# The last 32 tiles of a down-projection: from plain fp32 to three products of rounded parts and remainders

## The reference

```python
q = (xb @ w_q).reshape(tb, PEER_HEADS, 2, D_KEY // 2)
s = jnp.einsum('thpc,pnc->thpn', q, sub_keys).astype(jnp.float32)
...
gate = jax.nn.softmax(best_s, axis=-1)
pre = jnp.einsum('thkd,td->thk', u[expert], xb).astype(jnp.float32)
act = jax.nn.gelu(pre, approximate=False) * gate
return jnp.einsum('thk,thkd->td', act.astype(v.dtype), v[expert])
```

## Time and profile before

| what | value |
|---|---|
| median of 3 runs | 1876.55 us (1875.07 to 1878.01) |
| profiled execution, its own time | 1875.91 us |
| its span, first to last instruction | 1874.1 us |
| mean granted TensorE clock | 0.973 |
| PE, PEld, DVE busy | 95%, 81%, 77% of the span |
| ACT, POOL busy | 42%, 34% of the span |
| moved by DMA | 478.22 MB, mean 255 GB/s |
| the down-projection, first matmul to last | 1285.9 to 1860.4 us |

### The profile page before, as it was taken

One profiled execution on the slowest core, in us unless ns is written; L12 is line 12 of the kernel. 1 busy time (PEld: TensorE's weight loads), 2 busy tenths in 40 slices (PEclk: granted clock), 3 DMA queues, 4 the chain that ended last, 5 costly groups with the idle time before them and its releaser, 6 DMA issues.

```text
span 1874.1 us, 26361 instructions
## 1 busy us (share of the span) xinstructions
PE 1777.3 (95%) x9675; PEld 1516.0 (81%) x9675; DVE 1434.5 (77%) x2750; ACT 778.4 (42%) x1555; POOL 644.6 (34%) x409
## 2 busy tenths in 40 slices
PE   6999999989999899999999999978999999999997
PEld 6999776559998899999899999976676666766764
DVE  4433676665678788989999999867888788888787
ACT  3112566553444333333768788522222222222222
POOL 1100000000000133434223366555557566665672
PEclk8999799789999999999999999999999999999998
DMA  6233100002222589989788899999999999999996
GB/s 217 68 131 121 45 1 1 1 1 85 68 77 95 185 305 334 316 307 327 262 276 297 279 387 387 386 400 333 386 389 382 401 387 389 401 402 384 400 379 216
DMA packets 153599, 478.22 MB, mean 255 GB/s; under 512 B 14896, under 2 KB 53808, under 8 KB 149888
## 3 DMA queue, kind: packets, MB, share of 16 engines
q1 hardware_dynamic: 96112, 264.62, 38.7%
q0 software_dynamic: 56928, 208.28, 30.4%
q10 hardware_dynamic: 432, 3.64, 0.5%
HBM read 419.47 MB, written 56.75 MB: 254 GB/s over the span
## 4 chain that ended last, share of the span: by engine, by line
PE 69%; DVE 16%; DMA 8%; ACT 3%; issue 3%; POOL 0%; SPq 0%; ACTq 0%; DVEq 0%
PE ps L1003 17%; PE ps L981 16%; PE ps L633 10%; PE ps L1012 7%; PE ps L918 5%; DMA g_in<-gates_scattered 4%; PE ps L723 3%; DVE hot L1718 3%; DVE w_lo L1339 3%; DVE ring L1737 2%; PE ps L969 2%; PE ps L714 2%; PE ps L766 2%; DMA ring<-u_rows,idx_b 1%; DMA raw<-w_tiles 1%
## 5 line engine op out<-in xcount | busy, mean ns | idle before, releaser
L981 PE MATMUL ps<-md_hi,w_hi 128*128 128x384 f32 x1024 | 358.6, 350 | 36.9 <-DVE w_lo L1339 36.7
L981 PE MATMUL ps<-md_hi,w_lo 128*128 128x384 f32 x1024 | 345.8, 338 | 0.0
L981 PE MATMUL ps<-md_lo,w_hi 128*128 128x384 f32 x1024 | 345.7, 338 | 0.0
L613 POOL DMA_INDIRECT ring<-u_rows,idx_a x128 | 197.2, 1541 | 404.2 <-DVE dots L1737 294.8
L1339 DVE TENSOR_TENSOR w_lo<-raw,w_hi 128x1024 fp32r<-128x1024 f32 x176 | 215.3, 1223 | 79.2 <-ACT w_hi L1265 59.4
L613 POOL DMA_INDIRECT ring<-v_rows,idx_a x128 | 225.1, 1759 | 136.7 <-DVE acc L1747 105.4
L1737 DVE CUSTOM_DVE_ANT_0 ring<-ring,x_n 128x1024 f32<-128x1024 f32 x192 | 230.7, 1223 | 12.7 <-DMA ring<-u_rows,idx_b 10.7
L1747 DVE SCALAR_TENSOR_TENSOR acc<-ring,actg,acc 128x1024 f32<-128x1024 f32 x188 | 234.8, 1282 | 0.0
L981 PEld LDWEIGHTS ps<-md_hi,w_hi 128*128 128x128 f32 x1024 | 194.5, 190 | 46.3 <-DVE w_lo L1339 45.3
L1003 PE MATMUL ps<-w_hi,p_hi 128*128 128x512 f32 x576 | 193.0, 416 | 9.4 <-DVE w_lo L1805 9.1
L981 PEld LDWEIGHTS ps<-md_lo,w_hi 128*128 128x128 f32 x1024 | 194.5, 190 | 0.0
(11 more groups left out here) (265 smaller groups left out, 3261.2 us busy)
## 6 DMA issues: line engine op xcount, KB each, us to landing
raw<-w_tiles SPq DMA_DIRECT2D x176, 512.0 KB, 5.2
v_buf<-v_rows SPq DMA_DIRECT2D x128, 512.0 KB, 11.4
gates_scattered<-g_st SPq DMA_DIRECT2D x24, 1024.0 KB, 6.7
g_in<-gates_scattered SPq DMA_DIRECT2D x32, 768.0 KB, 15.8
activated<-act_st SPq DMA_DIRECT2D x112, 192.0 KB, 4.2
act_in<-activated SPq DMA_DIRECT2D x28, 768.0 KB, 12.9
kv_t<-qkv ACTq DMA_DIRECT2D x3, 1184.0 KB, 4.7
xh<-x_t SPq DMA_DIRECT2D x8, 296.0 KB, 6.0
```

The lines of the kernel that those rows point to most:

```text
L613: pool.indirect_dma_start(ring[slot][:], None, u_rows if table == "u" else v_rows, bass.IndirectOffsetOnAxis(ap=idx, axis=0)).then_inc(gat ...
L981: mm = nc.tensor.matmul(ps[:, slot, 0:ND], w[:, slot, kc, :], x[:, kc, :], start=(kc == 0 and j == 0), stop=(kc == KC - 1 and j == 2))
```

## The change

The list of split tiles becomes all 128 tiles, and the last split tile now closes the sums in PSUM. The plain branch (lines 1008 to 1015) is left in the code and no longer reached. Everything that asks `i in SPLIT` follows: `p_high` and `v_high` on ACT, `p_low` and `v_low` on DVE, the waits and the matmuls on PE. Order, buffers and transfers stay as they are.

```diff
-SPLIT = [i for i in range(N_EXP) if i % 4 != 3]
+SPLIT = list(range(N_EXP))
...
                                 mm = nc.tensor.matmul(ps[:, 2 + 2 * t + h, :], p[:, q % 3, t * P:(t + 1) * P],
                                                       v[q % 2][:, 512 * h:512 * h + 512],
-                                                      start=(i == 0 and n == 0), stop=False)
+                                                      start=(i == 0 and n == 0), stop=(i == N_EXP - 1 and n == 2))
```

## The result

The changed kernel takes 1889.03 us (median of 8 runs, 1880.85 to 1894.91) beside 1874.88 us for the kernel before on the same chip: a ratio of 1.0070, 95% interval [1.0049, 1.0091]. It is slower, by 0.3 to 0.7%; the two intervals don't meet, so the ratio of the same two kernels can differ by 0.4% between batches of runs. The profiled execution took 1885.29 us with a span of 1883.4, so 9.3 more than the span before.

What follows compares the result with a forecast made beforehand. PE was taken as the bound, with DVE's gates and near-saturated transfers close behind. Group ends -1.2, landing +5.4, clock +4.8 and first and last group -5.2 give +3.8 on 1875.9: 1879.7 us, range 1866 to 1891.

Steps and rivals of the forecast that it cites:

- Matmul term: PE in the down-projection: 32 plain tiles of 5.15 us become split tiles of 4.18, 31 us less matmul time.
- The new wait: Group ends: tile 15 waits for DVE's remainders behind late gates, PE waiting 3 to 6 us six times; net -1.2 us.
- Landing: Last gate piece of a group: lands 20.1 us after issue plus 0.9 for near-saturated transfers; +5.4 us, ends 0 and +11.6.
- sign of saturation: Gate transfers at group ends: a piece landing later than 21.5 us would show that transfers are saturated.
- The clock: PE after idle times at group ends: clock falls, costing 0.8 us a group; +4.8 us, ends 0 and +9.9.
- a sign read the wrong way: Argument against the slower rival: a PE that waits asks for less, so transfers catch up; no size of its own.
- The end: End of the last group: DVE's sums finish after PE, by 1.7 us, counted as +1.7.
- DVE and ACT at nothing between group ends: Between group ends: 51 us more on DVE and 50 on ACT hide in their idle time, costing nothing.
- Rows inside a group at nothing: Inside groups: PE's waits for rows cost nothing; such a wait would show the prediction wrong.
- The one on the slower side: Group ends: PE waits, landing unmoved, tile 15 at half clock, idle over about 5 us a group; 1891 us, chance 0.16.
- the forecast's own case: Whole kernel, the forecast's unknowns between their ends: 1873 to 1886 us, chance 0.56.
- The whole gain: Down-projection: gates land much sooner and PE stays the bound, 31 us less, about 1846 us; chance 0.08.

Runs made afterwards that it cites:

- e7: Changed kernel with the four gate pieces asked for at tiles 0, 2, 5 and 7 instead of 0, 3, 6 and 9: 1869.93 us, 0.9964.
- e4: Changed kernel plus four useless matmuls on PE ahead of the wait for tile 15's row remainder: 1879.24 us, 1.0014.
- e12: Changed kernel plus four useless matmuls ahead of the wait for tile 15's row remainder, on another chip: 1885.29 us, 1.0040.
- e5: Changed kernel loading only the first 512 columns of the rows from tile 6 on: 1842.92 us, 0.9826.
- e10: The changed kernel timed a second time, with no edit: 1883.42 us, 1.0028 to the kernel before.
- e9: Changed kernel with gates at tiles 0, 2, 5, 7, later residual loads and only the very last tile plain: 1864.01 us, 0.9930.
- e11: Kernel before (every fourth tile plain) with gates at tiles 0, 2, 5, 7 and later residual loads: 1870.86 us, 0.9975.
- e8: Changed kernel with gates at tiles 0, 2, 5, 7, each group's last tile plain and later residual loads: 1863.29 us, 0.9939.
- e3: Changed kernel with all four gate pieces asked for at tiles 0 to 3 of the group before: 1885.03 us, 1.0034.

## Why the prediction was right or wrong

The forecast was 1879.7 us, called no change; measured were 1889.03 and 1883.42, both within the range of 1866 to 1891. Both are slower, clear of their intervals, so the call of no change was missed by a little; slower had a chance of 0.38. By its steps:

- **Matmul term, right.** PE's busy time fell by 21.4 us; with the 11.1 that its clock took it would have fallen by 32.5, against 31 in the sum. In the chain nine split tiles in a row (18 matmuls each) took 37.92 us, 4.21 each, against 4.18 in the sum.
- **The new wait, right in place and cause.** At every group end in the chain but one, PE restarts 4.7 us after the gates land (1396.98 + 22.25 = 1419.23, then 1423.95), as worked out. The waits were said to be 3 to 6 us, six times; they were 1.0 to 7.7, six times.
- **Landing, right.** The six pieces in the chain landed after 22.25, 20.09, 18.00, 24.30, 22.51 and 19.60, 21.1 on average; taken were 20.1 + 0.9 = 21.0. One at 24.3 is past the 21.5 that was named as the sign of saturation.
- **The clock, mis-sized: the step that failed.** Taken were 0.8 us a group, with an upper end of 1.65; found were 11.1 / 6 = 1.85, past that end. The argument for 0.8 was that part of the loss is made up since transfers go on meanwhile. The trace shows that it isn't: from its first matmul to that of the next tile, tile 15 took 6.8, 5.7, 6.1, 5.8 and 7.0 us after the five long waits and 4.5 after the one of 1.0 us, where a split tile at full clock takes 4.18, and the next request for gates hangs on it. Behind the five long waits that is 10.5 us too much on PE's path, 1.75 a group. A group came to 74.2 us between requests where the terms give 71.4 + 0.9 + 0.8 = 73.1. Of the 1.05 between them 0.4 is landing, since the five pieces in these intervals took 21.4, and some 0.6 the clock; over all six group ends the landings come to what was taken, and the clock is what is left. Five such intervals make 5.3 of the 5.5 us between the +3.8 forecast and the +9.3 profiled.
- **Why nothing was made up: a sign read the wrong way.** The prediction knew that a PE that waits asks for less, and counted it as relief: transfers would catch up. They went on only until just after the gates were in. Then SP's loads were missing, which had waited for PE up to 13.1 us at the group end shown: 0.75 MB in ten us instead of 2.00. Transfers fell to 242 GB/s. That such stops are worth time is shown by e7, which ends the long ones and moves 396 GB/s; how much of the 9.3 us is the clock by itself and how much the thin queue behind the same stops, e4 and e12 leave open.
- **The end, right.** DVE's last sum stood 2.3 us behind PE (predicted 1.7):

```profile
1868.58 1.22 DVE L1845 TENSOR_TENSOR h_fin<-h_fin,acc 128x1024 f32<-128x1024 f32 x1
...
1869.72 3.67 DVE L1850 TENSOR_TENSOR h_fin<-ps,h_fin 128x512 f32<-128x512 f32 x6
```

- **DVE and ACT at nothing between group ends, right:** e5 has more of both and one wait of PE's after the start, of 0.5 us, before tile 75.
- **Rows inside a group at nothing, slightly wrong.** The prediction named a wait of PE for them as a sign against itself. It came: once in the last group, 1.0 us, and three times in e10, 5.4 us together.
- **The rivals.** The one on the slower side named the mechanism (a group's idle time over 5 us, and tile 15 at half clock): of the six idle times three were 4.3 or less, three 6.5 to 7.7, and the first timing, 1889, came out beside its 1891. The second, 1883, lies in the forecast's own case of 1873 to 1886. The whole gain, 1846, needed a rate above what the rows showed; only e5, with fewer bytes to move, came there.

## What to carry to other kernels

Where the busiest engine has a transfer close behind it, time the bytes first: a group's bytes over the rate that the trace shows, against the group's new compute time. If the bytes take longer, faster compute buys little but waits, and here long waits cost more than they lasted: the loads that wait for TensorE's tiles stopped with it, and it came back at half clock. Moving the pieces of a load to where the queue has room, neither late nor all at once, turned the same change from 0.3 to 0.7% slower into 0.4% faster (e7), and 0.7% with the residual's loads moved and the last tile left plain (e9); 0.25% of that the kernel before gains from the same moves (e11).

## What the runs showed of the hardware

- **No run moved more than some 400 GB/s for long.** Windows of 5 us reach 416 GB/s (1445 to 1450 us of the changed kernel); over 400 us the kernels move 383 (the change), 392 (before), 396 (e7), 397 (e9 and e11) and 399 (e8). The Trainium skill, DMA: Bandwidth & Descriptors, section Specifications, gives about 358 GB/s as a core's share of HBM; every one of these six runs is above it.
- **A load of one size can take very different times.** A piece of 768 KB of gates landed 10.2 to 24.3 us after its issue in the changed kernel (1320 to 1800 us). That this follows what stands ahead of it in the queue fits e3 and e7, but is not shown piece by piece.
- **The clock's fall came late in an idle time and outlasted it:** full up to 1641 us, 4.8 us into the idle time, then 1.2 GHz, and full again only from 1648, 4 us after PE was back at work.
